# Reading the moving tile of a matmul in two interleaved halves, in five of the stages of an encoder layer

## The chip, the cores and the metric

One core of a Trainium2 chip runs the whole layer as one program. The metric is the device time of that program in microseconds, the lower the better.

## The reference

One residual block over 256 tokens of 2048 channels, batch 1, in float32. Cut to what matters:

```
h    = rmsnorm(x, g_pre_mix)
proj = h @ w_in                    # 2048 -> 2*2048 + 2048 + 2048 + 16 + 3*2048 + 2*2048
hm   = head_rmsnorm(mlstm_chunkwise(silu(causal_dwconv(m_qk)), m_v, gates))   # 8 heads of 256
y_m  = (sigmoid(m_o) * hm) @ w_branch_m            # 2048 x 2048
ha   = head_rmsnorm(diff_attention(a_q, a_k, a_v)) * (1 - lam_init)
y_a  = ha @ w_branch_a                             # 2048 x 2048
mix  = (sigmoid(g_m) * y_m + sigmoid(g_a) * y_a) @ w_out     # 2048 x 2048
x    = x + rmsnorm(mix, g_post_mix)
h    = rmsnorm(x, g_pre_ffn)
u    = causal_dwconv(h @ w_up)                     # 2048 -> 2 * 5632, width 3
y    = (gelu(gate) * val) @ w_down                 # 5632 -> 2048
out  = x + rmsnorm(y, g_post_ffn)
```

## The kernel before

Every large product is made three times over. An fp32 number is split into `hi`, its rounding to fp32r (the format that TensorE reads at one column a cycle), and `lo`, the rest; then hi times hi, hi times lo and lo times hi are added in PSUM. The helper `three` issues these three matmuls (lines 1159 to 1161), `rows_unit` does the same with lines 1332 and 1336.

The weights come in **units** of 512 KB, 1024 columns for each of 128 partitions. SyncE loads a unit into one of four slots of `raw`, ScalarE rounds it into `w_hi` (line 540), VectorE subtracts to get `w_lo` (line 839), three units ahead of TensorE. The semaphores `raw_loaded`, `hi_done`, `lo_done` and `pe_done` pass a unit on; each engine's order is written out by hand.

There are five stages, one after the other:

- **mix**: 4 turns of 64 units, the input projection, with the attention and the mLSTM of two heads a turn woven in between. Most units are of the kind `unit_channels`: the weights are the stationary tile (128 channels), the activations `h_hi`, `h_lo` move, 256 tokens wide. Two of eight chunks are of the kind `unit_tokens`: activations stationary, weights moving, 512 wide.
- **branch**: 4 turns of 24 units, all `unit_channels`: eight with h (the gate), eight with hm, eight with ha.
- **output**: 4 turns of 8 units through `rows_phase` and `rows_unit`: the activations `ks_hi`, `ks_lo` are stationary and the weights move, 512 wide, into two banks of PSUM for each block of 128 tokens. In the last turn four of the units lie in `h`.
- **up**: 11 turns of 16 units, `unit_channels` with h.
- **down**: 11 turns of 8 units, `rows_phase` again.

A unit of the kind `unit_channels` is 2 x 4 x 3 = 24 matmuls of 256 columns; a unit of `rows_unit` is, for both token blocks, 12 matmuls of 512 columns.

Where a unit lies in its slot of `w_hi` and `w_lo` is a matter of three functions: `away(u)` puts it at the slot's start, `level_h(u)` moves it by 16 columns up or down, `level_ks(u)` by 0 or 32 columns. The slots are 1056 columns apart:

```
PITCH = UNIT + 32
def away(u):     return u % RING * PITCH
def level_h(u):  return u % RING * PITCH + (-16 if u % 2 else 16)
def level_ks(u): return u % RING * PITCH + (0 if u % 2 else 32)
```

The first three units of the output stage and of the down stage lie at `away`, the later ones at `level_ks`.

## Time and profile before

| | us |
|---|---|
| median of 2 runs | 1862.34 (1862.1 to 1862.58) |
| the profiled execution | 1862.29 |
| its span, first to last instruction | 1860.5 |
| TensorE busy | 1835.9 (99%) |
| VectorE busy | 1099.5 (59%) |
| ScalarE busy | 895.8 (48%) |
| mean granted clock of TensorE | 0.997 of 2.4 GHz |

The span is what the trace covers; the rest of the time is around it. A matmul's recorded duration goes from its start to the end of its last column and overlaps the next ones, so the distance between two starts, and not the duration, says how fast TensorE goes.

### The profile page before, as it was taken

The numbers are of one execution on the slowest core, as the hardware profiler recorded it, in microseconds if no ns is written. First come the engines' busy times: TensorE is split into PE (matmuls) and PEld (weight loads), VectorE is DVE, ScalarE is ACT, GpSimd is POOL, SyncE is SP. The second block draws the span as 40 slices with busy tenths as digits, with TensorE's granted clock in tenths as the row PEclk, the third lists the DMA queues.
The fourth block names the chain that finished last, engine by engine and source line by source line (L and its number), as shares of the span: only waits on it lengthen the run. The fifth ranks groups of instructions, "written<-read, shape, count | busy, mean of one in ns | idle before, by whom it ended". The sixth has DMA issues, their size and how long they took to land.

```text
span 1860.5 us, 35820 instructions
## 1 busy us (share of the span) xinstructions
PE 1835.9 (99%) x13768; PEld 1741.9 (94%) x13768; DVE 1099.5 (59%) x1311; ACT 895.8 (48%) x1161; POOL 72.1 (4%) x91
## 2 busy tenths in 40 slices
PE   7999999999999999999999998999999999999998
PEld 7999999999999999999999888999999999988886
DVE  5565556555655566545554557676666667755555
ACT  6444445444544454444434446555555555544443
POOL 5700000000000000000000000000000000000000
PEclk9999999999999999999999999999999999999999
DMA  7655655555556555555565664666666666565554
GB/s 227 205 180 170 193 179 176 173 189 180 181 170 192 182 172 181 183 195 193 188 195 197 250 203 132 197 194 193 197 194 191 192 192 192 192 215 193 194 193 142
DMA packets 164509, 351.53 MB, mean 189 GB/s; under 512 B 11049, under 2 KB 11329, under 8 KB 163777
## 3 DMA queue, kind: packets, MB, share of 16 engines
q1 hardware_dynamic: 162768, 344.11, 57.4%
q10 hardware_dynamic: 1280, 5.08, 0.7%
q0 software_dynamic: 368, 1.09, 0.2%
q8 instruction: 61, 1.00, 0.2%
q14 instruction: 32, 0.25, 0.0%
HBM read 348.12 MB, written 2.12 MB: 188 GB/s over the span
## 4 chain that ended last, share of the span: by engine, by line
PE 97%; DVE 1%; ACT 1%; issue 1%; DMA 0%; POOL 0%; DVEq 0%; SPq 0%; ACTq 0%; POOLq 0%
PE ps L1161 26%; PE ps L1159 26%; PE ps L1160 26%; PE ps L1332 11%; PE ps L1336 5%; PE ps L1222 1%; PE ps L1292 1%; DMA gm<-in_x 0%; PE ps L1230 0%; PE ps L1269 0%; DVE x L835 0%; ACT act L571 0%; ACT h L540 0%; PE ps L1268 0%; PE ps L1194 0%
## 5 line engine op out<-in xcount | busy, mean ns | idle before, releaser
L839 DVE TENSOR_TENSOR w_lo<-raw,w_hi 128x1024 fp32r<-128x1024 f32 x638 | 780.3, 1229 | 658.7 <-ACT w_hi L540 651.1
L540 ACT ACTIVATE w_hi<-raw 128x1024 fp32r<-128x1024 f32 x640 | 677.8, 1062 | 774.7 <-PE ps L1161 615.3
L1159 PE MATMUL ps<-h,w_hi 128*128 128x256 f32 x3200 | 886.6, 277 | 0.0
L1161 PE MATMUL ps<-h,w_lo 128*128 128x256 f32 x3200 | 883.8, 276 | 0.0
L1160 PE MATMUL ps<-h,w_hi 128*128 128x256 f32 x3200 | 883.8, 276 | 0.0
L1160 PEld LDWEIGHTS ps<-h,w_hi 128*128 128x128 f32 x3200 | 601.0, 188 | 0.5
L1159 PEld LDWEIGHTS ps<-h,w_hi 128*128 128x128 f32 x3200 | 601.0, 188 | 0.5
L1161 PEld LDWEIGHTS ps<-h,w_lo 128*128 128x128 f32 x3200 | 600.9, 188 | 0.0
L1332 PE MATMUL ps<-w_hi,ks_hi 128*128 128x512 f32 x448 | 174.6, 390 | 0.3 <-DVE ks_lo L835 0.2
L1336 PE MATMUL ps<-w_lo,ks_hi 128*128 128x512 f32 x448 | 174.3, 389 | 0.0
L1332 PE MATMUL ps<-w_hi,ks_lo 128*128 128x512 f32 x448 | 138.1, 389 | 0.0
L1332 PEld LDWEIGHTS ps<-w_hi,ks_hi 128*128 128x128 f32 x448 | 84.1, 188 | 18.2 <-issue 0.6
L1159 PE MATMUL ps<-w_hi,h 128*128 128x512 f32 x256 | 100.8, 394 | 0.0
L1332 PEld LDWEIGHTS ps<-w_hi,ks_lo 128*128 128x128 f32 x448 | 84.1, 188 | 17.7
L1336 PEld LDWEIGHTS ps<-w_lo,ks_hi 128*128 128x128 f32 x448 | 84.1, 188 | 17.4
L1160 PE MATMUL ps<-w_lo,h 128*128 128x512 f32 x256 | 99.7, 390 | 0.0
L1161 PE MATMUL ps<-w_hi,h 128*128 128x512 f32 x256 | 99.6, 389 | 0.0
L835 DVE SCALAR_TENSOR_TENSOR xn<-ps,chan,xn 128x254 f32<-128x254 f32 (+1 forms) x176 | 76.6, 477 | 26.4 <-ACT xn L792 19.3
L1159 PE MATMUL ps<-hm_hi,w_hi 128*128 128x256 f32 x256 | 70.7, 276 | 0.0
L1160 PE MATMUL ps<-hm_lo,w_hi 128*128 128x256 f32 x256 | 70.7, 276 | 0.0
L1161 PE MATMUL ps<-hm_hi,w_lo 128*128 128x256 f32 x256 | 70.7, 276 | 0.0
L1159 PE MATMUL ps<-ha_hi,w_hi 128*128 128x256 f32 x256 | 70.7, 276 | 0.0
(164 smaller groups left out, 1378.7 us busy)
## 6 DMA issues: line engine op xcount, KB each, us to landing
raw<-in_w_in SPq DMA_DIRECT2D x288, 512.0 KB, 3.5
raw<-in_w_up SPq DMA_DIRECT2D x176, 512.0 KB, 4.3
raw<-in_w_down SPq DMA_DIRECT2D x88, 512.0 KB, 4.4
raw<-in_w_branch_m SPq DMA_DIRECT2D x32, 512.0 KB, 4.5
raw<-in_w_branch_a SPq DMA_DIRECT2D x32, 512.0 KB, 4.4
raw<-in_w_out SPq DMA_DIRECT2D x32, 512.0 KB, 4.7
x<-in_x ACTq DMA_DIRECT2D x1, 2048.0 KB, 11.7
gm<-in_x SPq DMA_DIRECT2D x2, 512.0 KB, 4.7
```

The source lines that it names most:

```text
L540: return nc.scalar.activation(out_ap, in_ap, ACT.Copy, scale=scale)
L835: return nc.vector.scalar_tensor_tensor(out=out_ap, in0=in0, scalar=scalar, in1=in1, op0=op0, op1=op1)
L839: nc.vector.tensor_tensor(w_lo[:, at:at + UNIT], raw[:, slot, :], w_hi[:, at:at + UNIT].bitcast(F32), ALU.subtract).then_inc(lo_done, 1)
L1159: nc.tensor.matmul(out_ap, stat_hi, mov_hi, start=start, stop=False, skip_group_check=True)
L1160: nc.tensor.matmul(out_ap, stat_hi, mov_lo, start=False, stop=False, skip_group_check=True)
L1161: return nc.tensor.matmul(out_ap, stat_lo, mov_hi, start=False, stop=stop, skip_group_check=True)
L1222: last = nc.tensor.matmul(out_ap, weights[:, part * P:(part + 1) * P], v[:, s, j, 0:out_ap.shape[1]], start=i == 0, stop=i == len(parts) - 1)
L1292: last = nc.tensor.matmul(ps[:, 4 + j, (0, 256)[s]:(256, 384)[s]], kT[:, 2 * j + dt, s * P:(s + 1) * P], qT[:, 2 * j + dt, s * P:T], start ...
L1332: ins = nc.tensor.matmul(o, a, hi[:, n * 512:(n + 1) * 512], start=first and kslot == 0 and part is ks_hi, stop=last and kslot == 3 and pa ...
L1336: nc.tensor.matmul(o, a, lo[:, n * 512:(n + 1) * 512], start=False, stop=False, skip_group_check=True)
```

## The change

Five places hand a run length to a new helper `woven`. It splits the free dimension of an operand into two halves (a), each half into pieces of `run` columns (c), and takes piece 0 of the first half, piece 0 of the second half, piece 1 of the first half, and so on. It is put on the moving tile and on the PSUM output of the same matmul, so every product is added where it was before. The stationary tiles keep their patterns.

The run is 64 columns in the branch stage with h, 32 with hm, 8 with ha; 16 in the output stage; 16 in the up stage; 32 in the down stage. The mix stage passes no run and keeps its plain patterns, `unit_tokens` too. The two halves of a 256-column tile begin 128 columns (512 bytes) apart, those of a 512-column tile 256 columns (1024 bytes).

```diff
--- before.py
+++ after.py
@@ -1163,14 +1163,18 @@
             def ready(n):
                 pe.wait_ge(lo_done, n + 1 + RING)
 
-            def unit_channels(u, pair, a_hi_t, a_lo_t):
+            def woven(ap, run):
+
+                return ap.rearrange("p (a g c) -> p g a c", a=2, c=run) if run else ap
+
+            def unit_channels(u, pair, a_hi_t, a_lo_t, run=0):
 
                 for kk in range(2):
                     k = 2 * (u % UNITS_CHUNK) + kk
                     for t in range(4):
                         c = away(u) + kk * 512 + t * P
-                        last = three(ps[:, 2 * pair + t // 2, t % 2 * T:t % 2 * T + T],
-                                     w_hi[:, c:c + P], w_lo[:, c:c + P], a_hi_t[:, k, :], a_lo_t[:, k, :],
+                        last = three(woven(ps[:, 2 * pair + t // 2, t % 2 * T:t % 2 * T + T], run),
+                                     w_hi[:, c:c + P], w_lo[:, c:c + P], woven(a_hi_t[:, k, :], run), woven(a_lo_t[:, k, :], run),
                                      start=k == 0 and t % 2 == 0, stop=k == KT - 1)
                 last.then_inc(pe_done, 1)
 
@@ -1318,9 +1322,9 @@
                         pe.wait_ge(read_act, 6 * TURNS_MIX + 2)
                         pe.wait_ge(a_done, TURNS_MIX)
                     ready(g * U_BR + (BASE_BR + u))
-                    unit_channels(u, (2, 0, 1)[c], *((h_hi, h_lo), (hm_hi, hm_lo), (ha_hi, ha_lo))[c])
-
-            def rows_unit(u, b, first, last, banks=range(2)):
+                    unit_channels(u, (2, 0, 1)[c], *((h_hi, h_lo), (hm_hi, hm_lo), (ha_hi, ha_lo))[c], (64, 32, 8)[c])
+
+            def rows_unit(u, b, first, last, run, banks=range(2)):
 
                 kslot, half = rows_place(u, first or last)
                 at = away(u) if first and u < LOOKAHEAD else level_ks(u)
@@ -1328,16 +1332,16 @@
                 for part in (ks_hi, ks_lo):
                     for n in banks:
                         a = part[:, kslot, b * P:(b + 1) * P]
-                        o = ps[:, 4 * b + half * 2 + n, :]
-                        ins = nc.tensor.matmul(o, a, hi[:, n * 512:(n + 1) * 512],
+                        o = woven(ps[:, 4 * b + half * 2 + n, :], run)
+                        ins = nc.tensor.matmul(o, a, woven(hi[:, n * 512:(n + 1) * 512], run),
                                                start=first and kslot == 0 and part is ks_hi,
                                                stop=last and kslot == 3 and part is ks_lo, skip_group_check=True)
                         if part is ks_hi:
-                            nc.tensor.matmul(o, a, lo[:, n * 512:(n + 1) * 512],
+                            nc.tensor.matmul(o, a, woven(lo[:, n * 512:(n + 1) * 512], run),
                                              start=False, stop=False, skip_group_check=True)
                 return ins
 
-            def rows_phase(turns, per_turn, base, tiles_before, bank_waits):
+            def rows_phase(turns, per_turn, base, tiles_before, bank_waits, run):
                 def waits(g, u, first, last=False):
                     k, half = rows_place(u, first or last)
                     if first and k == 0:
@@ -1350,7 +1354,7 @@
                     for u in range(per_turn):
                         waits(g, u, first)
                         for b in range(TB):
-                            ins = rows_unit(u, b, first, False)
+                            ins = rows_unit(u, b, first, False, run)
                         ins.then_inc(pe_done, 1)
 
                 turn(0, True)
@@ -1362,7 +1366,7 @@
                     for u in range(c0 // HALF * RING, (c0 // HALF + 1) * RING):
                         if b == 0:
                             waits(turns - 1, u, False, True)
-                        ins = rows_unit(u, b, False, True, banks)
+                        ins = rows_unit(u, b, False, True, run, banks)
                         if i not in PIECES_EARLY:
                             ins.then_inc(pe_done, 1)
                     if i in PIECES_EARLY:
@@ -1376,7 +1380,7 @@
                 else:
                     pe.wait_ge(ba_read, TURNS_BR + 1)
 
-            rows_phase(TURNS_OUT, U_OUT, BASE_OUT, 0, out_banks)
+            rows_phase(TURNS_OUT, U_OUT, BASE_OUT, 0, out_banks, 16)
             early_tiles(xn, KT)
 
             def up_turn(g, first):
@@ -1393,7 +1397,7 @@
                         late_tiles(xn, KT, 12)
                         late_tiles(xn, KT, 14)
                     ready(g * U_UP + (BASE_UP + u))
-                    unit_channels(u, u // UNITS_CHUNK, h_hi, h_lo)
+                    unit_channels(u, u // UNITS_CHUNK, h_hi, h_lo, 16)
 
             up_turn(0, True)
             with pe.Fori(1, TURNS_UP) as g:
@@ -1402,7 +1406,7 @@
             def down_banks(half):
                 pe.wait_ge(*((gate_read, 2 * TURNS_UP + 1) if half == 0 else (val_read, TURNS_UP + 1)))
 
-            rows_phase(TURNS_DOWN, U_DOWN, BASE_DOWN, KT, down_banks)
+            rows_phase(TURNS_DOWN, U_DOWN, BASE_DOWN, KT, down_banks, 32)
 
 
 # ---- launch: one core
```

No instruction is added, removed or put elsewhere in any engine's order.

## Rows read from the trace of the kernel before

**Rows 1.** The page: busy time of the engines, and the granted clock.
```profile
span 1860.5 us, 35820 instructions
PE 1835.9 (99%) x13768; PEld 1741.9 (94%) x13768; DVE 1099.5 (59%) x1311; ACT 895.8 (48%) x1161; POOL 72.1 (4%) x91
...
PEclk9999999999999999999999999999999999999999
```

**Rows 2.** The page: the chain that ended last, by engine and by line.
```profile
PE 97%; DVE 1%; ACT 1%; issue 1%; DMA 0%; POOL 0%; DVEq 0%; SPq 0%; ACTq 0%; POOLq 0%
PE ps L1161 26%; PE ps L1159 26%; PE ps L1160 26%; PE ps L1332 11%; PE ps L1336 5%; PE ps L1222 1%; PE ps L1292 1%; DMA gm<-in_x 0%; PE ps L1230 0%; PE ps L1269 0%; DVE x L835 0%; ACT act L571 0%; ACT h L540 0%; PE ps L1268 0%; PE ps L1194 0%
```

**Rows 3.** The page: groups of matmuls; count, busy us, mean ns, idle before.
```profile
L1159 PE MATMUL ps<-h,w_hi 128*128 128x256 f32 x3200 | 886.6, 277 | 0.0
...
L1332 PE MATMUL ps<-w_hi,ks_hi 128*128 128x512 f32 x448 | 174.6, 390 | 0.3 <-DVE ks_lo L835 0.2
L1336 PE MATMUL ps<-w_lo,ks_hi 128*128 128x512 f32 x448 | 174.3, 389 | 0.0
L1332 PE MATMUL ps<-w_hi,ks_lo 128*128 128x512 f32 x448 | 138.1, 389 | 0.0
...
L1159 PE MATMUL ps<-hm_hi,w_hi 128*128 128x256 f32 x256 | 70.7, 276 | 0.0
...
L1159 PE MATMUL ps<-ha_hi,w_hi 128*128 128x256 f32 x256 | 70.7, 276 | 0.0
...
L1336 PE MATMUL ps<-h,ks_hi 128*128 128x512 f32 x32 | 12.5, 389 | 0.0
```

**Rows 4.** Windows of 100 us: branch, up and down stage.
```profile
core 0: us, PE busy (x) PEld busy (x) DVE busy (x) ACT busy (x) POOL busy (x), PEclk, DMA share, GB/s
850.00:950.00 100.00, 100.00 (x884) 100.00 (x884) 49.96 (x41) 40.51 (x40) 0.00 (x0) 1.00 0.59 194
1200.00:1300.00 100.00, 100.00 (x885) 100.00 (x884) 70.21 (x87) 53.15 (x63) 0.00 (x0) 1.00 0.61 192
1700.00:1800.00 100.00, 100.00 (x442) 82.80 (x442) 50.74 (x56) 45.10 (x56) 0.00 (x0) 1.00 0.58 192
```

**Rows 5.** Timeline, mix stage: one start and the twelfth after it (start us, duration us).
```profile
start us, us, engine line op out<-in xcount [idle before <-releaser]
300.13 0.28 PE L1160 MATMUL ps<-h,w_hi 128*128 128x256 f32 x1
...
301.49 0.28 PE L1160 MATMUL ps<-h,w_hi 128*128 128x256 f32 x1
```

**Rows 6.** Timeline, mix stage, after a change of kind: 24 matmuls between.
```profile
91.00 0.39 PE L1161 MATMUL ps<-w_hi,h 128*128 128x512 f32 x1
91.22 0.28 PE L1159 MATMUL ps<-h,w_hi 128*128 128x256 f32 x1
91.34 0.28 PE L1160 MATMUL ps<-h,w_hi 128*128 128x256 f32 x1
...
93.93 0.28 PE L1161 MATMUL ps<-h,w_lo 128*128 128x256 f32 x1
94.05 0.27 PE L1275 MATMUL ps<-shp,prob 128*128 128x128 f32 x1
```

**Rows 7.** Timeline, output stage: six matmuls in its first turn, six settled.
```profile
1037.26 0.40 PE L1332 MATMUL ps<-w_hi,ks_hi 128*128 128x512 f32 x1
...
1038.66 0.39 PE L1332 MATMUL ps<-w_hi,ks_hi 128*128 128x512 f32 x1
...
1070.04 0.39 PE L1332 MATMUL ps<-w_hi,ks_hi 128*128 128x512 f32 x1
...
1071.40 0.39 PE L1332 MATMUL ps<-w_hi,ks_hi 128*128 128x512 f32 x1
```

**Rows 8.** Timeline and group: fp32 matmuls of the attention.
```profile
102.89 1.24 PE L1222 MATMUL ps<-v,attnT 128*128 128x256 f32 x5
...
L1222 PE MATMUL ps<-v,attnT 128*128 128x256 f32 x48 | 11.0, 379 | 0.0
```

**Rows 9.** Waits in the up stage, 1140 to 1600 us: total, times, longest.
```profile
ACT w_hi L540 <- PE ps L1161: 187.8, 117, 1.7
DVE w_lo L839 <- ACT w_hi L540: 115.1, 95, 1.5
```

## The prediction

> **What bounds the kernel now.** I read the page's busy times first: the TensorE is busy 99% of the 1860.5 us span at a granted clock of nine tenths or more in all 40 slices, VectorE 59%, ScalarE 48% [rows 1]. The chain that ended last says the same: 97% of it is TensorE, the three lines of `three` and the two of `rows_unit` [rows 2]. So the time is the number of matmuls times the distance from one start to the next, and the question is only what the new access patterns do to that distance. The duration of a matmul in the groups of instructions (276 ns for 256 columns, 389 for 512 [rows 3]) isn't that distance, since matmuls overlap. The distance comes from two starts in the timeline: in the mix stage 12 matmuls of 256 columns start from 300.13 to 301.49 us, 1.36 / 12 = 113.3 ns each [rows 5]. It is the same in the stages that the change touches: the windows hold 884 and 885 matmuls in 100 us in the branch and the up stage, and 442 of 512 columns in 100 us in the down stage [rows 4], which is 100 / 882.4 = 113.3 ns and 100 / 441 = 226.7 ns once the one or two at the edges are taken off. The output stage has 1.36 / 6 = 226.7 ns as well, once it has settled [rows 7].
>
> Now set 113.3 ns against 256 columns. The full clock is 2.4 GHz, so 256 columns take 106.7 ns and 512 take 213.3. Measured are 6.7 and 13.3 ns more: exactly one cycle in 17, in proportion to the columns, in every stage, whichever tile moves (h, hm, ha or weights). It is no fixed cost of an instruction, since that wouldn't double with the columns, and no cost of the weight load beside it, since one load of 128 columns goes with either width. The matmuls that are fp32 and not fp32r have no such share: five in a row of the attention take 1.24 us, and less the last one's 0.38 that is 0.215 us for a pass of 256 columns, 213.3 at two cycles a column and some 2 ns [rows 8]. So the sixteenth belongs to a moving tile read at one 4-byte column a cycle.
>
> The trace also shows what a bad pair of addresses costs. After a change of kind, one whole unit of 24 matmuls takes from 91.22 to 94.05 us, 2.83 / 24 = 118 ns each, 4.6 above the settled pitch [rows 6]. In the first turn of the output stage, where the first three units lie at `away` and not at `level_ks`, six matmuls take 1.40 us, 233.3 ns each, 6.7 above the settled pitch [rows 7]. Same tiles, same columns, same clock: what differs is where the moving tile and the weights being loaded stand against each other. This matters because the change alters exactly the sequence of addresses of the moving tile.
>
> **The change part by part.** No instruction is added, removed or moved on any engine, no wait, no DMA. What changes is the order of the columns inside a matmul: `woven` turns one run of 256 (512) columns into 256 / run pieces that lie alternately in the first and the second half, for the moving tile and for PSUM alike, so each sum lands where it did and nothing that reads PSUM changes.
>
> How many matmuls: `unit_channels` makes 24 of them a unit. Branch stage, 4 turns of 8 units for each of three inputs: 768 with h in runs of 64, 768 with hm in runs of 32, 768 with ha in runs of 8. Up stage, 11 x 16 x 24 = 4224 in runs of 16. Together 6528 of 256 columns. Output, 4 x 8 x 12 = 384 of 512 columns in runs of 16; down, 11 x 8 x 12 = 1056 in runs of 32; together 1440. (The groups agree: 256 for each line with hm and with ha, and 448 + 32 for each of the three forms of `rows_unit` [rows 3].) At the settled pitch that is 6528 x 113.3 = 740 us and 1440 x 226.7 = 326 us, 1066 us of the 1860.5. The mix stage keeps its plain reads.
>
> Number of runs, which is the number of times that a stream jumps: 768 x (4 + 8 + 32) = 33,792 in the branch stage, 4224 x 16 = 67,584 in up, 384 x 32 = 12,288 in output, 1056 x 16 = 16,896 in down: 130,560.
>
> What does a jump cost? The trace of before has no jump inside an fp32r moving tile of these stages, so I bound it. From below: nothing, or less than nothing if the jump takes away a part of the sixteenth. From above: the nearest row is the sixteenth itself, one cycle of 0.417 ns in 16 columns; if a jump cost one such cycle on top, that is 130,560 x 0.417 = 54 us. I take nothing, by these reasons. Every run is at least 8 columns, 32 bytes, and starts at a multiple of 32 bytes, so no jump splits anything smaller than that, and the number of 32-byte pieces read and written is what it was. And the pitch today is the same for tiles at four different places, h, hm, ha and w, which says that the stream is limited by its rate, not by its address, except where two streams meet.
>
> What of two streams meeting? The cases of 118 and 233 ns show that it costs, at most 4.6 ns on 256 columns and 6.7 on 512. If all woven matmuls fell into it: 6528 x 4.6 = 30 us and 1440 x 6.7 = 10 us, 40 together. Against it: runs of 64 go through 256-byte stretches in the old order, and runs of 8 or 16 make the moving stream advance at half the speed, near that of the weights, which tends to hold the two apart once they are. In the trace a bad unit is followed by a good one without anything being done [rows 6, 5], the streams settle. I take nothing here as well, and keep 40 us as the bound.
>
> The other engines: ScalarE waits for TensorE to free a slot, 187.8 us in 117 waits in the up stage alone, and VectorE waits for ScalarE [rows 9]. Both are ahead, and TensorE waits for neither. A slower pitch leaves them more slack. A faster one by a seventeenth would take 6% from a unit of 2.72 us, 0.16 us, against waits of 187.8 / 117 = 1.6 us each; it would all be seen in the time.
>
> So the sum is 0 for 1066 us of work. The profiled execution took 1862.29 us, 1.8 around its span, and the median of before is 1862.34: I forecast 1862.3 us.
>
 No row of before tells between the two for TensorE; by the first rule the time is that of the first rival, by the others it stays.
>
> **The rivals.**
> *A jump costs a cycle, slower.* Place: the address walk of the moving tile or of PSUM's writes, at each run. Price: 54 us, so 1916.7 us, of which up has 28, branch 14, down 7, output 5. For it: the stream already loses a cycle per 16 columns to something that works in pieces. Against it: that something is the same for all tiles and no smaller piece appears. It decides (over 2%, 37 us) from 0.285 ns a jump, two thirds of a cycle.
> *The streams meet, slower.* Up to 40 us, 1902; half the stages in it, some 1882. For: 118 and 233 ns are real, and the placing at `level_ks` was right for plain reads. Against: settling.
> *The sixteenth goes, faster.* If the lost cycle comes from reading successive pieces of one stream, alternating between halves may hide it. With some 2 ns left per matmul as in the fp32 pass: 6528 x 4.7 = 31 us and 1440 x 11.4 = 16 us, so 1815 us; with nothing left, 1066 / 17 = 63 us, so 1800. If it works only in the up stage's runs of 16: 4224 x 4.7 = 20 us, 1842. For: the loss is there in 1066 us of work and goes with the stream. Against: it doesn't care about addresses now.
> *The change does nothing to the stream* because the pieces join up to one run again: they don't, neighbours are half a tile apart. It would give 1862 as well.
>
> **How the numbers follow.** No change 50%. A cycle a jump, or near it, 20%. Meeting streams 12%, a third of that over 2%. Faster 18%, of which 9 for all stages and 9 for some. Two per cent is about what a measurement of this kernel can tell from no change: under 1825 us I put 9%, over 1899.5 us 22%, between 69%. The range goes from 1842 (the up stage alone gains) to 1917 (a cycle a jump); outside are gains in all stages and jumps dearer than a cycle, some 14%. No change by itself would be 1860 to 1865.
>
> **What the profile of the changed kernel would show.** Number of matmuls in windows of 100 us in branch, up and down: 884, 885 and 442 if nothing changes. By the first rival the stages differ by run: ha 126.7 ns (32 jumps), up 120, hm 116.7, h 115, output 240, down 233.3; if h in runs of 64 and up in 16 show the same pitch, a cost per jump is refuted. By the second it would be 118 and 233 without regard to run, and in whole units. By the third it falls to 108.7 or 106.7. The mix stage should keep 113.3 in all cases. I would be wrong if a run shorter than some piece of the read path costs more than a cycle, which runs of 8 with ha would show first.

## The result: 54.6 us slower

| | before | after |
|---|---|---|
| median of 2 runs, us | 1862.34 | 1916.92 (1916.32 to 1917.53) |
| the profiled execution, us | 1862.29 | 1916.32 |
| its span, us | 1860.5 | 1914.5 |

The ratio is 1.0291, with a 95% interval of 1.0274 to 1.0307. The forecast was 1862.3, with a range from 1842 to 1917.

The page of the changed kernel first: busy times and clock, the chain that ended last by line, and the groups of matmuls (count, busy us and mean ns, idle before).

```profile
span 1914.5 us, 35820 instructions
...
PE 1890.4 (99%) x13768; PEld 1784.3 (93%) x13768; DVE 1100.5 (57%) x1311; ACT 898.6 (47%) x1161; POOL 72.2 (4%) x91
...
PEclk9999999999999999999999999999999999999999
...
PE ps L1159 26%; PE ps L1160 26%; PE ps L1161 26%; PE ps L1336 12%; PE ps L1340 6%; PE ps L1226 1%; PE ps L1296 1%; DMA gm<-in_x 0%; PE ps L1234 0%; PE ps L1273 0%; ACT h L540 0%; PE ps L1272 0%; PE ps L1198 0%; DVE x L835 0%; PE ps L1279 0%
...
L1159 PE MATMUL ps<-h,w_hi 128*128 128x256 f32 x3200 | 897.2, 280 | 0.0
...
L1336 PE MATMUL ps<-w_hi,ks_hi 128*128 128x512 f32 x448 | 179.8, 401 | 0.0
...
L1159 PE MATMUL ps<-ha_hi,w_hi 128*128 128x256 f32 x256 | 73.2, 286 | 0.0
...
L1159 PE MATMUL ps<-hm_hi,w_hi 128*128 128x256 f32 x256 | 72.2, 282 | 0.0
```

The instruction counts are those of before, the clock is full, and the same lines hold the chain [rows 1, 2]. VectorE's busy time is 1100.5 us after 1099.5, ScalarE's 898.6 after 895.8. So all that grew is on TensorE: 1890.4 - 1835.9 = 54.5 us, the whole difference. And it grew matmul by matmul: a group with ha has a mean of 286 ns and one with hm 282, where both had 276 [rows 3]; for the line with `ks_hi` of `rows_unit` it is 401 for 390.

Then windows of 20 us of the changed kernel, in this order: h, hm and ha in the branch stage, output, up, down. The columns are those of [rows 4].

```profile
774.00:794.00 20.00, 20.00 (x179) 20.00 (x178) 9.69 (x8) 8.25 (x8) 0.00 (x0) 1.00 0.62 200
795.00:815.00 20.00, 20.00 (x170) 20.00 (x169) 8.58 (x7) 8.43 (x9) 0.00 (x0) 1.00 0.55 186
818.00:838.00 20.00, 20.00 (x165) 20.00 (x164) 9.20 (x8) 6.76 (x7) 0.00 (x0) 1.00 0.56 184
1080.00:1100.00 20.00, 20.00 (x85) 15.87 (x84) 9.43 (x11) 8.63 (x11) 0.00 (x0) 1.00 0.58 202
1200.00:1220.00 20.00, 20.00 (x169) 20.00 (x168) 11.49 (x13) 7.07 (x9) 0.00 (x0) 1.00 0.58 183
1700.00:1720.00 20.00, 20.00 (x86) 16.02 (x85) 9.58 (x10) 8.46 (x11) 0.00 (x0) 1.00 0.53 184
```

A matmul is counted if any part of it lies in the window, so the starts spread over the window and the duration of one matmul. For 256 columns that is (20 + 0.28) / 179 = 113.3 ns with h, 119.3 with hm, 20.29 / 165 = 123.0 with ha and 20.28 / 169 = 120.0 in the up stage; for 512 it is (20 + 0.40) / 85 = 240.0 in the output stage and 20.40 / 86 = 237.2 in the down stage. One count more or less is 0.7 ns, so where it matters I take two starts in the timeline of the changed kernel, 60 matmuls apart with hm and with ha, 72 apart in the down stage:

```profile
796.94 0.28 PE L1160 MATMUL ps<-hm_lo,w_hi 128*128 128x256 f32 x1
...
804.07 0.28 PE L1160 MATMUL ps<-hm_lo,w_hi 128*128 128x256 f32 x1
```
```profile
819.86 0.28 PE L1160 MATMUL ps<-ha_lo,w_hi 128*128 128x256 f32 x1
...
827.26 0.28 PE L1160 MATMUL ps<-ha_lo,w_hi 128*128 128x256 f32 x1
```
```profile
1699.98 0.40 PE L1336 MATMUL ps<-w_hi,ks_hi 128*128 128x512 f32 x1
...
1717.02 0.40 PE L1336 MATMUL ps<-w_hi,ks_hi 128*128 128x512 f32 x1
```

That is 7.13 / 60 = 118.8 ns (118.9 before rounding the starts), 7.40 / 60 = 123.3 and 17.04 / 72 = 236.7. The list of the stages, against 113.3 and 226.7 of before [rows 4, 7]:

| stage | run, columns | ns | above before | matmuls | us |
|---|---|---|---|---|---|
| branch, h | 64 | 113.3 | 0 | 768 | 0 |
| branch, hm | 32 | 118.9 | 5.6 | 768 | 4.3 |
| branch, ha | 8 | 123.3 | 10.0 | 768 | 7.7 |
| output | 16 | 240.0 | 13.3 | 384 | 5.1 |
| up | 16 | 120.0 | 6.7 | 4224 | 28.2 |
| down | 32 | 236.7 | 10.0 | 1056 | 10.6 |

The sum is 55.9 us, against 54.6 measured. In both traces, from the first matmul of a stage to the first of the next, the mix stage takes 749.6 us before and 749.7 after, the branch stage 261.5 and 273.5, the output stage 98.4 and 102.8, and the up stage 480.5 and 507.9. So the mix stage kept its time, the branch stage grew by 12.0 us as the table says, and output and up grew by 4.5 and 27.5 us, a little less than it says. Before, their first units were above the settled pitch: the four first of the output stage had 228 to 239 ns, and the first of the up stage 140 ns, after the change 124.

What waits for TensorE waited longer, as the waits of the changed kernel in 460 us of its up stage show (total us, times, longest), in answer to [rows 9]:

```profile
ACT w_hi L540 <- PE ps L1161: 204.0, 122, 1.8
DVE w_lo L839 <- ACT w_hi L540: 130.9, 90, 1.7
```

The total is just above that of the rival "a jump costs a cycle", 1916.7, but the shape is not its own. By it a run of 64 would have cost 1.7 ns and a run of 8 13.3; measured are 0 and 10.0. A run of 32 has half the jumps of a run of 16 and costs nearly the same, 5.6 ns and 6.7. By cycles of 0.417 ns, 120.0 ns is 288 for 256 columns: a second sixteenth on top of the first.

### The profile page after: what moved, and what is told of

It reads as the page before. It is cut to its first block, busy times and chain, and to the rows that moved or that the text cites. A ratio compares the mean times of both kernels' runs of the same rounds, so it can differ in the third digit from the quotient of the medians.

```text
span 1914.5 us, 35820 instructions
## 1 busy us (share of the span) xinstructions
PE 1890.4 (99%) x13768; PEld 1784.3 (93%) x13768; DVE 1100.5 (57%) x1311; ACT 898.6 (47%) x1161; POOL 72.2 (4%) x91
## 4 chain that ended last, share of the span: by engine, by line
PE 97%; issue 1%; DVE 1%; ACT 0%; DMA 0%; POOL 0%; SPq 0%; DVEq 0%; ACTq 0%; POOLq 0%
PE ps L1159 26%; PE ps L1160 26%; PE ps L1161 26%; PE ps L1336 12%; PE ps L1340 6%; PE ps L1226 1%; PE ps L1296 1%; DMA gm<-in_x 0%; PE ps L1234 0%; PE ps L1273 0%; ACT h L540 0%; PE ps L1272 0%; PE ps L1198 0%; DVE x L835 0%; PE ps L1279 0%
## 5 line engine op out<-in xcount | busy, mean ns | idle before, releaser
L1159 PE MATMUL ps<-h,w_hi 128*128 128x256 f32 x3200 | 897.2, 280 | 0.0
L1160 PE MATMUL ps<-h,w_hi 128*128 128x256 f32 x3200 | 894.3, 279 | 0.0
L1161 PE MATMUL ps<-h,w_lo 128*128 128x256 f32 x3200 | 894.1, 279 | 0.0
L1336 PE MATMUL ps<-w_hi,ks_hi 128*128 128x512 f32 x448 | 179.8, 401 | 0.0
L1340 PE MATMUL ps<-w_lo,ks_hi 128*128 128x512 f32 x448 | 179.1, 400 | 0.0
L1336 PE MATMUL ps<-w_hi,ks_lo 128*128 128x512 f32 x448 | 143.1, 400 | 0.0
L1161 PE MATMUL ps<-ha_hi,w_lo 128*128 128x256 f32 x256 | 73.2, 286 | 0.0
L1160 PE MATMUL ps<-ha_lo,w_hi 128*128 128x256 f32 x256 | 73.2, 286 | 0.0
```

Of the source, the lines that this page charges most:

```text
L1159: nc.tensor.matmul(out_ap, stat_hi, mov_hi, start=start, stop=False, skip_group_check=True)
L1160: nc.tensor.matmul(out_ap, stat_hi, mov_lo, start=False, stop=False, skip_group_check=True)
L1161: return nc.tensor.matmul(out_ap, stat_lo, mov_hi, start=False, stop=stop, skip_group_check=True)
L1336: ins = nc.tensor.matmul(o, a, woven(hi[:, n * 512:(n + 1) * 512], run), start=first and kslot == 0 and part is ks_hi, stop=last and kslot ...
L1340: nc.tensor.matmul(o, a, woven(lo[:, n * 512:(n + 1) * 512], run), start=False, stop=False, skip_group_check=True)
```

## The experiments

Two things had changed, the read of the moving tile and the write of PSUM, and there were two theories of the price. The **jump theory**: each jump costs, more or less a cycle. The **place theory**: what counts is in which order the stream visits the places that repeat every 256 bytes (64 columns); runs of 64 keep that order, shorter ones come back to a place too soon. Each expectation below was written before its kernel ran. Three chips were used, one for each group of kernels, and each group has its own runs of the kernel before: 1862.71 (e1 to e4), 1862.97 (e5 to e7) and 1863.09 us (e8, e9).

### e1 and e2: the reads alone, the writes alone

`plain` keeps the four dimensions of the pattern but in the natural order, since the two patterns of a matmul have to have one shape. e1 has it in place of `woven` on PSUM, e2 on the moving tile:

```
 def plain(ap, run):
     return ap.rearrange("p (g a c) -> p g a c", a=2, c=run) if run else ap
e1:  three(plain(ps[...], run), ..., woven(a_hi_t[:, k, :], run), woven(a_lo_t[:, k, :], run), ...)
     o = plain(ps[:, 4 * b + half * 2 + n, :], run)
e2:  three(woven(ps[...], run), ..., plain(a_hi_t[:, k, :], run), plain(a_lo_t[:, k, :], run), ...)
     nc.tensor.matmul(o, a, plain(hi[:, n * 512:(n + 1) * 512], run), ...)
```

> The moving tiles are read in the two interleaved halves as in the changed kernel, while PSUM is written in plain order, so the products land in permuted columns and the result is another one. If the cost sits in the read of the moving tile: 1917 us, up stage 120 ns a matmul, ha 123, hm 119, down 236.7. If it sits in PSUM's writes: 1862 us and 113.3 / 226.7 ns everywhere. If both sides share it: between.

> The other half alone: PSUM is written in interleaved halves, the moving tiles are read plainly (permuted result). Read theory: 1862 us, nothing moves. PSUM theory: 1917 us with 120 ns in the up stage.

Measured: e1 1916.92 us, ratio 1.0292 [1.0275, 1.0309]; e2 1862.94, ratio 1.0001 [0.9992, 1.0011]. Windows with ha, in the output, the up and the down stage, first e1:

```profile
818.00:838.00 20.00, 20.00 (x164) 20.00 (x163) 9.11 (x8) 6.69 (x8) 0.00 (x0) 1.00 0.63 184
1080.00:1100.00 20.00, 20.00 (x85) 15.85 (x84) 9.43 (x11) 8.64 (x11) 0.00 (x0) 1.00 0.60 193
1200.00:1220.00 20.00, 20.00 (x169) 20.00 (x169) 11.41 (x13) 7.07 (x9) 0.00 (x0) 1.00 0.62 183
1700.00:1720.00 20.00, 20.00 (x86) 15.98 (x85) 9.59 (x10) 8.46 (x11) 0.00 (x0) 1.00 0.58 184
```

and e2:

```profile
818.00:838.00 20.00, 20.00 (x179) 20.00 (x179) 9.71 (x9) 7.44 (x7) 0.00 (x0) 1.00 0.68 196
1080.00:1100.00 20.00, 20.00 (x90) 16.57 (x89) 10.79 (x12) 8.36 (x10) 0.00 (x0) 1.00 0.62 198
1200.00:1220.00 20.00, 20.00 (x179) 20.00 (x178) 14.59 (x18) 11.74 (x14) 0.00 (x0) 1.00 0.64 196
1700.00:1720.00 20.00, 20.00 (x90) 16.57 (x89) 10.54 (x12) 8.66 (x11) 0.00 (x0) 1.00 0.62 195
```

With the reads woven each stage has the pitch of the changed kernel; with the writes woven all have that of before. All of the time is in the read of the moving tile, and PSUM takes 130,560 jumps, in runs down to 8 columns, for nothing. Of the two rules of the Trainium skill that the prediction set against each other, the one in PSUM — Partial Sum Buffer (Specifications), that any non-contiguous pattern slows matmuls, is not borne out by the writes here. Advanced Engine Details and Errata (PSUM Cachelines) repeats that rule and also asks for every two consecutive elements to be contiguous; with this second sentence the trace agrees. e2 also says that a PSUM pattern of four dimensions has no price as such.

### e3: other runs in the same stages

```
-  ((h_hi, h_lo), (hm_hi, hm_lo), (ha_hi, ha_lo))[c], (64, 32, 8)[c])
+  ((h_hi, h_lo), (hm_hi, hm_lo), (ha_hi, ha_lo))[c], (8, 16, 64)[c])
-  rows_phase(TURNS_OUT, U_OUT, BASE_OUT, 0, out_banks, 16)
+  rows_phase(TURNS_OUT, U_OUT, BASE_OUT, 0, out_banks, 64)
-  unit_channels(u, u // UNITS_CHUNK, h_hi, h_lo, 16)
+  unit_channels(u, u // UNITS_CHUNK, h_hi, h_lo, 64)
-  rows_phase(TURNS_DOWN, U_DOWN, BASE_DOWN, KT, down_banks, 32)
+  rows_phase(TURNS_DOWN, U_DOWN, BASE_DOWN, KT, down_banks, 64)
```

> The run lengths of the changed kernel exchanged: up, output and down in runs of 64, branch h in 8, hm in 16, ha in 64. Theory that every jump costs about a cycle: up has 4 jumps instead of 16, so 115 ns, output and down (8 jumps) 230 ns, in all about 1862 + 29 = 1891 us with branch h 126.7. Theory of places (what counts is how soon the stream comes back to the same 64-byte stretch, taken modulo 256 bytes; halves lie 512 or 1024 bytes apart, so runs of 64 go through these stretches in the plain order): up 113.3, output and down 226.7, ha 113.3, hm 120, h 123.3, so 1862.3 + 768 x 6.7 + 768 x 10 ns = 1875 us. Theory that the tile's place decides and not the run: h in the branch would stay at 113.3 and ha at 123.

Measured: 1875.69 us, ratio 1.0069 [1.0052, 1.0086]. Windows with h in runs of 8, hm in 16, ha in 64, then up in 64 and down in 64:

```profile
773.00:793.00 20.00, 20.00 (x164) 20.00 (x163) 8.58 (x7) 8.03 (x8) 0.00 (x0) 1.00 0.61 188
797.00:817.00 20.00, 20.00 (x169) 20.00 (x169) 8.58 (x7) 8.25 (x9) 0.00 (x0) 1.00 0.57 184
820.00:840.00 20.00, 20.00 (x178) 20.00 (x177) 9.59 (x9) 7.84 (x8) 0.00 (x0) 1.00 0.65 188
1200.00:1220.00 20.00, 20.00 (x179) 20.00 (x178) 13.20 (x17) 10.10 (x12) 0.00 (x0) 1.00 0.59 167
1700.00:1720.00 20.00, 20.00 (x90) 16.55 (x89) 10.47 (x12) 8.36 (x11) 0.00 (x0) 1.00 0.58 192
```

h is now the slow one (123.3 ns) and ha the fast one (20.28 / 178 = 113.9, with the change of chunk in it). So the price belongs to the run and not to the tile. Runs of 64 are free in three tiles and at both widths: the up stage has four jumps a matmul and the down stage eight, 4224 x 4 + 1056 x 8 = 25,344 jumps, and neither lost a nanosecond. The sum of the branch stage is 768 x 10.0 + 768 x 6.7 = 12.8 us, against 13.0 measured. The place theory's time is right, the jump theory's not.

### e4: 21 ways to read one tile

In the mix stage the activations of six chunks in each of four turns are read by a form (pieces, run): the tile is cut into that many equal parts, which are read in turn, `run` columns of each. The five stages behind are those of the kernel before.

```
+ def woven(ap, form):
+     return ap.rearrange("p (a g c) -> p g a c", a=form[0], c=form[1]) if form else ap
+ FORMS = {(0, 0): (2, 64), (0, 1): (2, 32), (0, 3): (2, 16), (0, 4): (2, 8), ...}   # (turn, chunk)
-                        unit_channels(u, c % 2, h_hi, h_lo)
+                        unit_channels(u, c % 2, h_hi, h_lo, FORMS.get((g, c)))
```

> The kernel before, with the 19 chunks of the mix stage's four turns that follow each in a form of its own (a parts of 256/a columns, taken in turn in runs of c), all moving the same h: a=2 with c=64,32,16,8,4,2; a=4 with 32,16,8,4,2; a=8 with 16,8,4,2; a=16 with 8,4,2; a=32 with 4,2; a=64 with 2; three chunks plain. Cost per jump: the pitch depends on c alone, (2,16), (4,16), (8,16) all 120, (2,8), (4,8), (8,8), (16,8) all 123. Theory of places: (2,64) 113.3, (2,32) 119, (2,16) 120, (2,8) 123, but (4,16) dearer than (2,16), about 123, because four pieces in a row lie in the same stretch modulo 256 bytes, (8,16) about 119 (back after two), and (16,8), (16,4), (16,2) at 113.3 or less, since each next piece is in the next 64-byte stretch.

Measured: 2003.55 us in one execution. Windows of (2, 2) and (4, 16):

```profile
197.00:217.00 20.00, 20.00 (x122) 19.98 (x121) 8.76 (x10) 6.63 (x9) 0.00 (x0) 1.00 0.42 120
252.00:272.00 20.00, 20.00 (x170) 20.00 (x169) 8.58 (x7) 8.30 (x9) 0.00 (x0) 1.00 0.64 185
```

That is 20.34 / 122 = 166.7 and 20.28 / 170 = 119.3 ns.

The mean distances, ns for 256 columns (from starts in the timeline, over whole units):

| pieces | run 64 | 32 | 16 | 8 | 4 | 2 |
|---|---|---|---|---|---|---|
| 2 | 113.3 | 118.9 | 120.0 | 123.3 | 126.6 | 169 |
| 4 | | 120.1 | 119.3 | 120 | 136 | 226 |
| 8 | | | 121 | 117.1 | 124 | 231 |
| 16 | | | | 118.6 | 115 | 220 |
| 32 | | | | | 119 | 233 |
| 64 | | | | | | 229 |

For runs of 64 to 8 the first row is what the changed kernel showed, in other stages. The rest speaks against both theories in their simple form. A cost per jump would make each column of the table one number, and make it fall to the left: (16, 4) has 64 jumps and 115 ns, (2, 16) has 16 jumps and 120.0. And the simple place theory, in which the price depends on how soon the stream comes back to a place, had expected 123 for (4, 16), 119 for (8, 16) and at most 113.3 for the forms of 16 pieces; they gave 119.3, 121, and 118.6, 115 and 220. What does stand out is the run of 2 columns: close to two distances in one, whatever the number of pieces, except with two. The Trainium skill, in SBUF — State Buffer (Specifications, the row on cachelines), has lines of 16 bytes and full bandwidth from two accesses to a line on. By that, runs of 4 columns and more would cross no more lines than a plain read and be as fast, and runs of 2 would just reach the two accesses: the trace disagrees on both, with 126.6 ns for (2, 4) and 169 for (2, 2).

The means hide one thing. In this stage the weights of successive units lie at 0 and at 32 columns modulo 64 in turn, and in several forms the pitch changes with them. Three units of (8, 8), one behind the other, begin so:

```profile
457.52 0.28 PE L1159 MATMUL ps<-h,w_hi 128*128 128x256 f32 x1
...
460.28 0.27 PE L1159 MATMUL ps<-h,w_hi 128*128 128x256 f32 x1
...
463.14 0.28 PE L1159 MATMUL ps<-h,w_hi 128*128 128x256 f32 x1
```

That is 2.76 / 24 = 115.0 ns with the weights at 0 and 2.86 / 24 = 119.2 with them at 32. (4, 8), (16, 8) and (32, 4) change by 1.5 to 4.2 ns from unit to unit, higher with the weights at 0, and (16, 4) has 113.3 ns in every fourth unit. So for these forms a part of the price depends on how the read stands against the weights.

### e5: the order of places, by hand-made steps

Here the steps are written out, so that the number of jumps and the order of places can be chosen apart. Each form has 256 columns in pieces of `run`, every second piece at a distance D behind the one before it. PSUM is written in the natural order.

```
+ FORMS = {(0, 0): (0, [[32, 8], [16, 2], [1, 16]]),    # run 16, D 16: the natural order
+          (0, 1): (0, [[32, 8], [32, 2], [1, 16]]),    # run 16, D 32
+          (0, 6): (0, [[32, 8], [80, 2], [1, 16]]), ... # run 16, D 80
+ def moving(ap, form):
+     return bass.AP(ap.tensor, ap.offset + form[0], [list(ap.ap[0])] + form[1]) if form else ap
```

> The kernel before, with 21 chunks of the mix stage reading h by hand-made steps, PSUM in plain order; the halves overlap or leave columns out, so the products of these chunks are other ones and only their pitch is read. Theory of places (the stream pays by how soon it comes back to a place modulo 256 bytes, jumps as such are free): runs of 16 whose second piece lies 16 + 64 or 16 + 128 columns on, and runs of 8, 4, 32 with 8 + 64, 4 + 64, 32 + 64, go through the 256 bytes in plain order with a jump at each piece and stay at 113.3 ns; runs of 64 with the second half 144, 160 or 176 columns on, instead of 128, leave that order and cost more than 113.3; reading the same 16 columns sixteen times is the dearest, over 120. Theory of run length (whatever is shorter than 256 bytes in one piece costs, wherever it lies): the first group costs as in the sweep, 120 for 16, 123 for 8, 127 for 4, 119 for 32, and the runs of 64 stay at 113.3 at any distance. A start one or two columns into a 16-byte line: both say near 113.3.

Measured: 1878.62 us in one execution. Windows of the chunks with run 16 and D = 16, 32, 144, then run 8 with D = 72, run 4 with D = 68, and run 32 with D = 160:

```profile
24.00:44.00 20.00, 20.00 (x178) 20.00 (x177) 12.98 (x14) 12.20 (x15) 16.10 (x14) 1.00 0.69 220
47.00:62.00 15.00, 15.00 (x130) 15.00 (x129) 8.00 (x6) 5.40 (x6) 14.00 (x13) 1.00 0.58 188
192.00:210.00 18.00, 18.00 (x161) 18.00 (x161) 10.79 (x12) 8.72 (x11) 0.00 (x0) 1.00 0.54 172
214.00:234.00 20.00, 20.00 (x179) 20.00 (x178) 8.93 (x8) 8.92 (x9) 0.00 (x0) 1.00 0.65 199
236.00:256.00 20.00, 20.00 (x179) 20.00 (x178) 9.25 (x8) 8.61 (x9) 0.00 (x0) 1.00 0.63 196
404.00:424.00 20.00, 20.00 (x169) 20.00 (x168) 8.58 (x7) 8.24 (x9) 0.00 (x0) 1.00 0.59 186
```

By the same working as above: 20.28 / 178 = 113.9 (113.3 once the first unit is past), 15.28 / 130 = 117.5, 18.28 / 161 = 113.5, then 20.28 / 179 = 113.3 twice, and 20.28 / 169 = 120.0. With run 64 and D = 160, two starts in the timeline, 42 matmuls apart, 5.04 / 42 = 120.0 ns:

```profile
354.32 0.28 PE L1159 MATMUL ps<-h,w_hi 128*128 128x256 f32 x1
...
359.36 0.28 PE L1159 MATMUL ps<-h,w_hi 128*128 128x256 f32 x1
```

All forms but the two late starts, from such starts:

| run | next pair after | D, columns | order of places modulo 64 columns | ns |
|---|---|---|---|---|
| 16 | 32 | 16 | natural, no jump | 113.3 |
| 16 | 32 | 80, 144 | natural, a jump after every run | 113.3 |
| 8, 4, 32 | 16, 8, 64 | 72, 68, 96 | natural, a jump after every run | 113.3 |
| 16 | 32 | 32, 48, 64 | not natural | 117.8, 118.8, 118.8 |
| 32 | 32 | 160 | not natural | 120.2 |
| 32 | 32 | 64 | not natural | 118.8 |
| 64 | 64 | 144, 160, 176 | not natural | 118.3, 120.0, 118.0 |
| 16 | 16 | 144, 160, 176 | not natural | 120.7, 122.8, 120.0 |
| 64 | 0 | 0 | natural, the same 64 each time | 113.3 |
| 16 | 0 | 0 | not natural, the same 16 each time | 121 |

One thing was missed: a plain read that starts 1 or 2 columns late, in the natural order, has 119 and 120.5 ns where 113.3 was expected. So a natural order isn't enough. e6 and e8 took that up.

### e6 and e8: where the weights lie

While a matmul reads its moving tile, the weights of the next are loaded from the same memory: the loads were busy 93% of the span of the changed kernel, under matmuls that were busy 99% of it. The prediction had read 118 and 233 ns as a bad meeting of the two [rows 6, 7]. Does the woven order cost by itself, or by such a meeting? Both kernels leave 96 columns between the slots of `w_hi` and `w_lo` in place of 32, which gives room to shift the weights. In e6 the chunks are at `away`, at `level_h` or at `level_ks`, the turns are plain, (2, 16), (2, 32), and the fourth loads 64 or 32 columns of weights in place of 128. In e8 the weights' places modulo 64 columns are as in the table below, and the turns plain, (2, 16), (2, 64), and plain with the activations read 4 columns late.

```
-PITCH = UNIT + 32
+PITCH = UNIT + 96
e6:  return (away, level_h, level_h, level_ks, away, level_h, level_h, level_ks)[u % U_MIX // UNITS_CHUNK](u)
     three(woven(ps[0:m, ...], form), w_hi[:, c:c + m], w_lo[:, c:c + m], ...)      # m = 128, 64 or 32
e8:  c = u % U_MIX // UNITS_CHUNK
     if c == 0: return away(u)
     return u % RING * PITCH + (0 if u % 2 else 32) + {1: -16, 2: -16, 3: 0, 4: 16, 5: -16, 6: -32, 7: -24}[c]
     bass.AP(ap.tensor, ap.offset + shift, [list(p) for p in ap.ap])                # shift = 4, fourth turn
```

> The kernel before with slots 1120 columns apart, the weights of the mix stage's chunks at three places in their slots (0, +-16, 32 columns), three turns in three forms (plain, halves in runs of 16, in runs of 32), and in the fourth turn stationary tiles of 64 or 32 columns instead of 128, which leaves out part of the outputs; the 512-column chunks take forms too. Theory that the moving stream pays alone: plain 113.3, runs of 16 120.0 and of 32 119 at every place of the weights and with 64 or 32 stationary columns as well; 512 wide, runs of 128 and 64 226.7, 32 some 237, 16 240. Theory that the two streams meet (moving tile against the weights being loaded): the pitch changes with the place of the weights by 4 ns and more, and falls towards 109 where only 64 or 32 columns are loaded.

> The kernel before with slots 1120 columns apart and the weights of the mix stage's chunks held at fixed places modulo 64 columns: chunk 0 alternating 0 and 32 as before, chunk 1 at 16 (the place of h itself), 3 at 32, 4 at 48, 6 at 0, 7 at 8; turns: plain, halves in runs of 16, halves in runs of 64, plain but read from 4 columns (one 16-byte line) further on, which reads a shifted tile. Theory of two conditions (order of places modulo 256 bytes kept, and the weights well placed): plain and runs of 64 agree with each other at every place, 113.3 in chunk 0, 120.0 in chunk 1, and between in the others; runs of 16 are at 120.0 in all six. If the order were all that counts: plain and runs of 64 at 113.3 in all six. A start 4 columns on: near the plain value if whole lines are what matters, 118 to 120 if the distance from the weights must be a multiple of 16 columns.

Measured: e6 1888.5 us, e8 1881.38, one execution each. Windows of e8, first the chunks with weights at 0 and 32 in turn and at 16, plain:

```profile
25.00:43.00 18.00, 18.00 (x161) 18.00 (x160) 11.25 (x10) 11.13 (x12) 15.25 (x13) 1.00 0.73 230
46.00:66.00 20.00, 20.00 (x169) 20.00 (x168) 9.58 (x7) 8.16 (x8) 18.44 (x19) 1.00 0.58 185
216.00:236.00 20.00, 20.00 (x169) 20.00 (x169) 9.64 (x8) 7.43 (x7) 0.00 (x0) 1.00 0.61 187
410.00:428.00 18.00, 18.00 (x161) 18.00 (x160) 8.58 (x7) 7.26 (x8) 0.00 (x0) 1.00 0.60 191
432.00:452.00 20.00, 20.00 (x169) 20.00 (x168) 9.15 (x8) 7.55 (x8) 0.00 (x0) 1.00 0.60 185
```

The first two rows and the last two are chunk 0, with the weights at 0 and 32 in turn, and chunk 1, with them at 16: plain, then in runs of 64. The third row is chunk 0 in runs of 16. In ns: 18.28 / 161 = 113.5 and 120.0 for plain, 20.28 / 169 = 120.0 for runs of 16, and 113.5 and 120.0 again for runs of 64. The rest from starts in the timeline:

| weights at, modulo 64 | plain | runs of 64 | runs of 16 | plain, 4 columns late |
|---|---|---|---|---|
| 0 and 32 in turn | 113.3 | 113.3 | 120.0 | 119 |
| 16 (where h is) | 120.0 | 120.0 | 120.0 | 116.7 |
| 32 | 113.3 | 113.3 | 120.0 | 119.2 |
| 48 | 118.7 | 118.7 | 120.0 | 118.7, then 116.7 |
| 0 | 117.8, then 113.3 | 117.8, then 113.3 | 120.0 | 118.4, then 120.0 |
| 8 | 116.7 | 116.7 | 120.0 | 118.3 |

The change to 113.3 in the row of 0 comes after four units, where other matmuls of the mix stage are put in between.

Three things follow. A plain read too has a price, by where the weights lie against it: from 113.3 to 120.0 ns, so 113.3 is what the kernel before gets by its placing, not what a matmul costs anywhere. Runs of 64 are the same as plain unit by unit, in the bad places also. And runs of 16 cost 120.0 at every place: exactly plain's worst. No placing of the weights that I tried gives anything back for runs of 16.

In e6 plain reads had 113.3 ns at `away`, 120.0 at `level_h`, and at `level_ks` 113.3 in one chunk and 117.8 in another; runs of 16 had 120.0 in all six chunks, runs of 32 118.9. In its fourth turn runs of 16 stayed at 120.0 ns with 64 and with 32 columns of weights loaded, and plain reads had 116.7 and 118.7 in turn with 64 columns and 113.3 with 32, once the first two units were past. Runs of 64 with 64 columns of weights had 113.3 ns in their first units and 119.0 in their last. Windows of e6, runs of 16 with 64 columns and plain with 32:

```profile
629.00:649.00 20.00, 20.00 (x169) 20.00 (x168) 8.64 (x8) 8.07 (x8) 0.00 (x0) 1.00 0.57 182
704.00:724.00 20.00, 20.00 (x179) 19.02 (x177) 16.34 (x25) 11.16 (x15) 0.00 (x0) 1.00 0.57 179
```

Runs of 16 with 32 columns, two starts in the timeline, 42 matmuls apart, 5.04 / 42 = 120.0 ns:

```profile
749.29 0.28 PE L1159 MATMUL ps<-h,w_hi 128*32 128x256 f32 x1
...
754.33 0.28 PE L1159 MATMUL ps<-h,w_hi 128*32 128x256 f32 x1
```

If the 120.0 of the woven order were its meeting with the weights, a quarter of the weights should have changed it. It didn't, which speaks for a cost of the order by itself in runs of 16; it isn't proof, since 32 columns of weights are still loaded once a matmul, and (8, 8) of e4 does change with the weights. e6 also had weights as the moving tile of 512 columns: 226.7 ns for runs of 128 and 64, 236.7 for 32, 240.0 for 16, 233.3 for (4, 32), 231.1 for (4, 16) and 236.7 for (8, 32), of which the figures for halves in runs of 32 and 16 are those of the down and the output stage of the changed kernel.

### e7 and e9: the changed kernel with the up stage plain, and with all stages in runs of 64

```
e7: -  unit_channels(u, u // UNITS_CHUNK, h_hi, h_lo, 16)
    +  unit_channels(u, u // UNITS_CHUNK, h_hi, h_lo)
e9: the run is 64 in all five calls, in place of (64, 32, 8)[c], 16, 16 and 32
```

> The changed kernel with the up stage alone back at plain reads. If each stage pays its own matmuls and nothing is given back elsewhere: 4224 x 6.67 ns = 28.2 us less than 1916.9, so 1888.7 us. If a part of the cost sits in waits that the slower pitch brings, less would come back than the up stage's own pitch says.

> The changed kernel with runs of 64 columns in all five stages, as many woven matmuls as in the changed kernel and a right result. Theory of places: the whole 54.6 us come back, 1862.3 us, although every woven matmul of 256 columns still jumps 4 times and one of 512 columns 8 times. Cost per jump: 7968 woven matmuls with 37,632 jumps, at 0.417 ns 15.7 us, so 1878 us.

Measured: e7 1889.86 us, ratio to before 1.0144 [1.0127, 1.0161]. It is 26.9 us above the kernel before in its own group of runs, where the changed kernel was 54.6 above in its own. So the up stage alone is worth 54.6 - 26.9 = 27.7 us, for 28.2 from the pitches and 27.5 from the starts of the stages. e9: 1862.93 us, ratio 0.9997 [0.9988, 1.0007]. Windows of e9, output, up, down:

```profile
1080.00:1100.00 20.00, 20.00 (x90) 16.57 (x89) 10.52 (x12) 8.36 (x10) 0.00 (x0) 1.00 0.60 195
1200.00:1220.00 20.00, 20.00 (x179) 20.00 (x178) 14.57 (x18) 11.93 (x14) 0.00 (x0) 1.00 0.64 192
1700.00:1720.00 20.00, 20.00 (x90) 16.57 (x89) 10.54 (x12) 8.66 (x11) 0.00 (x0) 1.00 0.59 196
```

All 7968 matmuls of the change read two halves in turn, and the time is that of before. With the change's own runs it is 1916.92. So the whole 54.6 us hang on the length of the runs against 64 columns.

## Why the prediction was wrong

**What bounds the kernel: right.** TensorE's pitch was the time. All 54.6 us are in it, and no other engine came near.

**The pitch and the counts: right.** 113.3 and 226.7 ns, 6528 and 1440 matmuls, 130,560 jumps: the sum of the stages, with the new pitches in it, is within 1.3 us of the result.

**The cost of a jump, taken as nothing: the step that failed.** I had reasoned that "position within a larger power of two up to the run's length is also what it was at every point of the stream: whatever in the memory goes round by position sees the old sequence up to 32 bytes at least". The sentence is correct, and it is even the right kind of rule, since e5 shows that what counts is position within a power of two. But I let 32 bytes pass for enough with no row that said so. The power is 256 bytes. By it the step would have read: h in runs of 64 is free and the five other readings are not, and at the price of the bad rows of before, 4.6 and 6.7 ns, (6528 - 768) x 4.6 + 1440 x 6.7 = 36 us. The runs gave 55.9 by the pitches, since the price is 5.6 to 10.0 ns on 256 columns and 10.0 to 13.3 on 512.

**"Limited by its rate, not by its address": wrong.** It rested on four tiles with one pitch. All four were read in the natural order and lay at well-placed addresses. Three of them even lay at one place for this purpose: by the built kernel of before `h`, `hm_hi` and `ha_hi` all begin 16 columns behind the start of `w_hi`, modulo 64. e8 gives plain reads 113.3 to 120.0 by address. Equal numbers from four cases that share the property in question say nothing about the property.

**Streams that meet, and settle: half right.** A plain read does pay by where the weights lie, up to 120.0 ns (e8). But place alone doesn't settle it: one chunk of e8 has 117.8 in four units and then 113.3 with the weights at the same place modulo 64 columns. That bad units become good by themselves was read from [rows 6, 5], which stand 206 us apart and don't show it; the trace of before does: the chunk that begins at 91.2 us has 117.8 and 117.7 ns in its first two units and 113.3 in the third, with nothing between the second and the third. And I took the settling of plain reads for a property of woven ones. Woven runs of 16 don't settle: they stay at 120.0 ns from unit to unit.

**The rivals.** "A jump costs a cycle" had the best time, 1916.7 for 1916.92, by a wrong mechanism: e3 has 25,344 jumps for nothing, and e5 64 a matmul for nothing. Its table of stages was off by -1.7 (h), +2.2 (hm), 0 (up), -3.4 (ha), 0 (output) and +3.4 ns (down), and the errors cancelled. "The streams meet" had the sizes nearly right and their distribution wrong, since they go by run. "The sixteenth goes" is the opposite of what happens: a second one comes. The prediction's own test, h in runs of 64 and up in 16 at one pitch, came out the other way (113.3 and 120.0), which alone would have left a cost per jump standing; it took e3 and e5 to refute it.

**PSUM's writes: right to cost them at nothing** (e2), against the first of the two rules that the prediction had set against each other.

**Still open.** What in the read path makes the order modulo 256 bytes count; why forms that break it cost 2 to 13 ns (23 once, and 56 to 120 with runs of 2) with no order that I could find in e4's table, and how much of that is a meeting with the weights, since some of them change with the weights' place and halves in runs of 16 don't; why one and the same place of the weights modulo 64 columns has 113.3 in one chunk of e6 and 117.8 in another; why a sixteenth stays even at best. No kernel here went under 113.3 ns, and no version beats the kernel before.

## What to carry to other kernels

A moving tile that is read in an order other than the natural one is free if each jump lands where the stream would have been next modulo 256 bytes (64 columns of fp32r), however many jumps there are, provided the plain read at that place was good too. Otherwise reckon, for two halves in runs of 8 to 32 columns, with 4 to 9% on every matmul of a kernel that TensorE bounds. PSUM was written in two interleaved halves, in runs of 8 columns and up, for nothing. And before "it is the same for all tiles" is taken as proof that addresses don't count, see whether the tiles differ in the property that the change alters.

## What was not expected of the hardware

- With fp32r and weights loaded anew for each matmul, 256 columns take 113.3 ns at best at the full clock. Plain reads take up to 120.0 when only the weights are placed otherwise modulo 64 columns (e8).
- A start 1, 2 or 4 columns late costs up to 7 ns on 256 columns (e5: 119 and 120.5; e8: 116.7 to 120).
- Runs of 2 columns take 220 to 233 ns, nearly double, but 169 if there are only two pieces (e4).
- Loading 32 columns of weights in place of 128 doesn't lower 113.3 ns (e6).
